# Third mixer: attention units from the ninth tile's slot, the last value tile projected in halves, sinks and first turned copies by ScalarE

## The chip, the core and the metric

The kernel runs on one core of a Trainium2 chip. The metric is the device time of one execution in microseconds (us), median of several; the profile is of one execution.

## What is computed

Four decoder layers over 512 tokens of width 1024 in float32. Each adds a token mixer and then a gated FFN to the residual stream. The change touches only layer 3's mixer, sliding-window attention with sinks (16 query heads, 4 key and value heads of 64, window 128):

```python
q = _partial_rope(_rmsnorm(q, q_norm), cos, sin)
k = _partial_rope(_rmsnorm(k, k_norm), cos, sin)
scores = jnp.einsum('bnqhgd,bnkhd->bnhgqk', qb, kw) * (hd ** -0.5)
scores = jnp.where(mask[None, :, None, None], scores, -jnp.inf)
m = jnp.maximum(jnp.max(scores, axis=-1, keepdims=True), sink)
p = jnp.exp(scores - m)
denom = jnp.sum(p, axis=-1, keepdims=True) + jnp.exp(sink - m)
o = jnp.einsum('bnhgqk,bnkhd->bnqhgd', p / denom, vw).reshape(bsz, s, nq)
return o.astype(h.dtype) @ w_out
```

## The kernel before

Every float32 product with weights is made of two matmuls: a high part in fp32r (`w1`, `x1` or `y1`) and a low part in bf16 (`w2`, `x2` or `y2`). Weights come in panels of 128 x 1024 by DMA from SyncE into a ring of four; ScalarE makes a panel's high part (line 251), GpSimd its low part in four pieces (line 281), and TensorE uses both. A panel slot's high part is made again when TensorE has used the panel four before it.

The mixer's input projection has 12 tiles of 128 features by 512 tokens, one panel each: two of keys (0, 1), eight of queries (2 to 9), two of values (10, 11). A tile is 8 high matmuls (line 310) and 8 low ones (line 320). VectorE scales it out of PSUM (line 2482, an "eviction"), ScalarE squares it, TensorE makes the sums for the head norm ("stat", line 2329), and VectorE applies the rotary embedding ("rope", lines 2498 to 2504: a shuffle into PSUM bank 4, two products, a sum).

Attention runs in 16 units: unit `un` is query tile `un // 2` and a half `un % 2` of the token blocks. An even unit has one short key range (128 keys), so its scores and turns are smaller. The steps of one unit are
- score: TensorE multiplies queries and keys (line 2345); VectorE masks, scales and takes the maximum in four reductions (line 2531); ScalarE makes four exponentials with their sums (line 2441). VectorE first writes the sinks beside the scores (line 2523).
- weights: VectorE takes the reciprocal of the unit before (line 2509), in the midst of the reductions; GpSimd multiplies by it (line 2564).
- turn: TensorE transposes the rows into banks 7 and 4 (line 2362); ScalarE copies bank 7 (line 2455), VectorE bank 4 (`second`, line 2541).
- pv: TensorE multiplies with the values (line 2381); every second unit ScalarE makes `y1` (`high`, line 2461) and VectorE `y2` (`low`, line 2547).
- early: one matmul pair of the output projection (lines 351 and 359), 14 in all.

Values are first turned by TensorE (`turn_v`, line 2318) and copied by ScalarE (line 2423), which counts `swa_v`. The product of an even unit waits for `swa_v`: unit 0 for one, later even ones for both.

The order is written out by hand in `swa_events`: a list of slots, which each engine walks and from which it takes its own steps. Engines take their steps strictly in that order and wait on semaphores. In slot n stands tile n; the statistics and the rope of a tile stand one slot later. Unit v stands in slot `SWA_FIRST + v`; there its score, the turn of unit v - 2 and the product of unit v - 3. The turn of unit 0 waits for all ropes (`swa_rotated` at 30), as bank 4 holds the ropes' partner rows. Buffers for scores rotate over three; the third shares its space with the rope's scratch `xc`.

## Time and profile before

| | us |
|---|---|
| median of 3 runs | 1725.84 (1725.24 to 1725.88) |
| the profiled execution | 1724.62 |
| its span | 1722.8 |
| TensorE busy | 1685.2 (98%) |
| VectorE, ScalarE, GpSimd busy | 1142.7, 1098.6, 1233.2 |

The third mixer stands from 901 to 1013 us. A timeline lists an engine's instructions in order of time: start and duration in us, engine, line and operation, output and inputs, how many were merged, and in brackets the idle time before and who ended it. Ends of matmuls are modelled and groups overlap by their tails, so prices of TensorE's parts are read from start to start; some matmul records are missing.

### The profile page before, as it was taken

The numbers are of one execution on the slowest core, as the hardware profiler recorded it, in microseconds if no ns is written. First come the engines' busy times: TensorE is split into PE (matmuls) and PEld (weight loads), VectorE is DVE, ScalarE is ACT, GpSimd is POOL, SyncE is SP. The second block draws the span as 40 slices with busy tenths as digits, with TensorE's granted clock in tenths as the row PEclk, the third lists the DMA queues.
The fourth block names the chain that finished last, engine by engine and source line by source line (L and its number), as shares of the span: only waits on it lengthen the run. The fifth ranks groups of instructions, "written<-read, shape, count | busy, mean of one in ns | idle before, by whom it ended". The sixth has DMA issues, their size and how long they took to land.

```text
span 1722.8 us, 26957 instructions
## 1 busy us (share of the span) xinstructions
PE 1685.2 (98%) x9549; PEld 1054.9 (61%) x9708; DVE 1142.7 (66%) x1965; ACT 1098.6 (64%) x1566; POOL 1233.2 (72%) x1776
## 2 busy tenths in 40 slices
PE   7999999999999999999999999999999999999999
PEld 4556666666566556666665666666666665566665
DVE  6986777228888865777328857775248886677720
ACT  7887666456877756666545776665455665866632
POOL 7867777877556648777887657778766554777786
PEclk9999999999999999999999999999999999999999
DMA  7334444546233225444544124444443332444443
GB/s 275 113 99 129 150 149 143 157 149 182 74 98 99 97 86 169 149 147 146 156 144 142 38 69 141 150 149 150 146 133 99 99 99 75 134 147 146 147 155 127
DMA packets 65614, 226.53 MB, mean 131 GB/s; under 512 B 8149, under 2 KB 9045, under 8 KB 65109
## 3 DMA queue, kind: packets, MB, share of 16 engines
q1 hardware_dynamic: 64236, 221.89, 40.9%
q10 hardware_dynamic: 1245, 2.92, 0.6%
q8 instruction: 78, 1.28, 0.3%
q14 instruction: 55, 0.45, 0.1%
HBM read 222.48 MB, written 2.10 MB: 130 GB/s over the span
## 4 chain that ended last, share of the span: by engine, by line
PE 78%; ACT 7%; DVE 7%; issue 3%; POOL 3%; DMA 1%; SPq 0%; DVEq 0%; ACTq 0%; POOLq 0%
PE psum L310 24%; PE psum L320 23%; PE psum L351 13%; PE psum L359 12%; POOL w_rest L281 2%; ACT w_big L251 1%; DVE psum L1670 1%; PE psum L2345 1%; PE psum L2381 1%; ACT psum L1514 1%; ACT L1549 1%; DMA w_panel<-in_ssd_in 1%; ACT L1530 1%; PE psum L2362 1%; DVE arena L1715 1%
## 5 line engine op out<-in xcount | busy, mean ns | idle before, releaser
L281 POOL TENSOR_TENSOR w_rest<-w_panel,w_big 128x256 bf16<-128x256 f32 x1660 | 1170.5, 745 | 415.6 <-ACT w_big L251 415.2
L310 PE MATMUL psum<-x_big,w_big 128*128 128x512 f32 x2248 | 590.8, 409 | 7.6 <-ACT x_big L410 6.2
L251 ACT ACTIVATE w_big<-w_panel 128x1024 fp32r<-128x1024 f32 (+1 forms) x414 | 417.0, 1032 | 181.5 <-PE psum L359 124.0
L320 PE MATMUL psum<-x_rest,w_rest 128*128 128x512 bf16 x2141 | 501.2, 380 | 9.2 <-DVE x_rest L513 1.9
L310 PEld LDWEIGHTS psum<-x_big,w_big 128*128 128x128 f32 x2248 | 418.4, 189 | 117.0 <-issue 14.0
L320 PEld LDWEIGHTS psum<-x_rest,w_rest 128*128 128x128 bf16 x2248 | 205.6, 98 | 267.4 <-issue 41.0
L750 DVE SCALAR_TENSOR_TENSOR psum<-ffn_raw,params,psum 128x512 f32<-128x512 f32 x352 | 264.5, 751 | 7.2 <-ACT psum L704 1.0
L742 DVE TENSOR_TENSOR ffn_raw<-psum,rstd 128x512 f32<-128x512 f32 x176 | 120.4, 686 | 140.8 <-PE psum L320 131.8
L704 ACT ACTIVATE psum<-ffn_raw,params 128x512 f32<-128x512 f32 x176 | 137.3, 782 | 99.9 <-DVE ffn_raw L742 95.6
L580 DVE SCALAR_TENSOR_TENSOR x_resid<-psum,x_resid 128x512 f32<-128x512 f32 x64 | 43.8, 688 | 219.7 <-PE psum L359 211.7
L351 PE MATMUL psum<-g_big,w_big 128*128 128x512 f32 x704 | 183.2, 411 | 0.0
L359 PE MATMUL psum<-g_rest,w_rest 128*128 128x512 bf16 x678 | 158.2, 380 | 1.5
L351 PEld LDWEIGHTS psum<-g_big,w_big 128*128 128x128 f32 x704 | 132.7, 189 | 34.2
L711 ACT ACTIVATE g_big<-psum 128x512 fp32r<-128x512 f32 x88 | 52.8, 600 | 112.2 <-DVE psum L759 112.1
L359 PEld LDWEIGHTS psum<-g_rest,w_rest 128*128 128x128 bf16 x704 | 65.0, 98 | 86.1 <-issue 14.3
L351 PE MATMUL psum<-y_big,w_big 128*128 128x512 f32 x320 | 106.6, 457 | 0.5 <-ACT w_big L251 0.5
L513 DVE SCALAR_TENSOR_TENSOR x_rest<-x_big,psum 128x512 bf16<-128x512 f32 x64 | 44.0, 687 | 90.8 <-ACT psum L414 90.8
L359 PE MATMUL psum<-y_rest,w_rest 128*128 128x512 bf16 x298 | 83.0, 382 | 1.4 <-POOL w_rest L281 0.8
L351 PEld LDWEIGHTS psum<-y_big,w_big 128*128 128x128 f32 x320 | 60.2, 191 | 16.3 <-issue 4.1
L759 DVE TENSOR_TENSOR psum<-psum,ffn_silu_out 128x512 f32<-128x512 f32 x88 | 61.5, 699 | 3.2
L763 DVE SCALAR_TENSOR_TENSOR g_rest<-g_big,psum 128x512 bf16<-128x512 f32 x88 | 59.9, 680 | 2.7 <-ACT g_big L711 2.7
L1670 DVE SCALAR_TENSOR_TENSOR psum<-arena,params,psum 128x512 f32<-128x512 f32 x72 | 54.3, 754 | 10.8 <-ACT psum L1514 9.1
(281 smaller groups left out, 1646.5 us busy)
## 6 DMA issues: line engine op xcount, KB each, us to landing
w_panel<-in_up SPq DMA_DIRECT2D x176, 512.0 KB, 3.5
w_panel<-in_dn SPq DMA_DIRECT2D x64, 448.0 KB, 3.2
w_panel<-in_ssd_in SPq DMA_DIRECT2D x41, 512.0 KB, 3.5
w_panel<-in_dn SPq DMA_DIRECT2D x32, 512.0 KB, 3.5
w_panel<-in_hgrn_in SPq DMA_DIRECT2D x32, 512.0 KB, 3.5
w_panel<-in_lru_in SPq DMA_DIRECT2D x18, 512.0 KB, 3.5
w_panel<-in_ssd_out SPq DMA_DIRECT2D x16, 512.0 KB, 3.4
w_panel<-in_swa_in SPq DMA_DIRECT2D x12, 512.0 KB, 3.4
```

Source lines behind the costliest of these rows:

```text
L251: act.activation(k.w1[:, slot, 0:words], k.w[:, slot, 0:words], ACT.Copy, scale=(SHIFT - 1) / SHIFT).then_inc(k.s("panel_big"), 1)
L281: rest = pool.tensor_tensor(k.w2[:, slot, a], k.w[:, slot, a], k.w1[:, slot, a].bitcast(F32), ALU.subtract)
L310: pe.matmul(out, k.w1[:, slot, q * m:(q + 1) * m], k.x1[:, q, :], start=q == 0, stop=False)
L320: mm = pe.matmul(out, k.w2[:, slot, q * m:(q + 1) * m], k.x2[:, q, :], start=False, stop=q == DT - 1)
L351: pe.matmul(out, k.w1[:, slot, (q - p0) * P:(q - p0 + 1) * P], y1[:, q, :], start=q == 0, stop=False)
L359: mm = pe.matmul(out, k.w2[:, slot, (q - p0) * P:(q - p0 + 1) * P], y2[:, q, :], start=False, stop=q == kt - 1)
L704: act.activation(out, k.ffn_raw[:, j % 2, half, 2:], ACT.Identity, bias=k.p("ffn_conv_b", j + (l * 2 * FF_T + half * FF_T)), scale=k.p("ff ...
L742: dve.tensor_tensor(k.ffn_raw[:, j % 2, half, 2:], k.ps[:, k.bank(job, i), :], k.rstd[:, :], ALU.mult).then_inc(k.s("banks_free"), 1)
L750: dve.scalar_tensor_tensor(out, k.ffn_raw[:, j % 2, half, tap:tap + S], k.p("ffn_conv_w", j + ((l * 3 + tap) * 2 * FF_T + half * FF_T)), o ...
L759: dve.tensor_tensor(out, out, k.ffn_silu[:, j % 2, :], ALU.mult).then_inc(k.s("ffn_gated"), 1)
L763: dve.scalar_tensor_tensor(k.g2[:, j, :], k.g1[:, j, :].bitcast(F32), 1 - SHIFT, k.ps[:, lin_bank(j), :], ALU.mult, ALU.add).then_inc(k.s( ...
L1670: dve.scalar_tensor_tensor(conv, b.raw[:, i % 2, tap:tap + S], k.p("ssd_conv_w", tap * 24 + ch), conv, ALU.mult, ALU.add).then_inc(k.s("ss ...
```

## The change

- `SWA_FIRST` goes from 9 to 8: unit v stands in slot 8 + v. In the first two of these slots the rope comes behind the unit's score instead of ahead of it.
- Value tile 11 has no slot of its own: its high half stands in slot 11, between the scores and the product of a unit, its low half in slot 12. The two value turns stand behind the turns of unit 0 and of unit 2. ScalarE's rounding of the panel behind it (`last_round`) stands at the end of slot 12, just ahead of the second value copy.
- The sinks are written by ScalarE, a unit ahead, at a slot's end, and no longer by VectorE.
- For units 0 to 2 (`SWA_BOTH`) ScalarE makes both turned copies.
- The rope's scratch `xc` moves to the last plane of `y`, and unit 2's reductions no longer wait for all ropes.
- An early step takes its low matmul first and then the high one.
- GpSimd weights unit 0 behind panel 12, unit 1 behind 13, units 2 to 5 behind 14, unit 6 within 15.

```diff
@@ -2200,10 +2200,8 @@
         self.vt = a.take(NC, 256)
         self.vraw = a.take(2, S)
         self.scores = [a.take(2, 2, 260) for _ in range(2)]
-        at = a.at
         self.scores.append(a.take(2, 2, 260))
-        roped = Arena(k, at)
-        self.xc = roped.take(S)
+        self.xc = k.y[:, SSD_T - 1, :]
         self.pt = a.take(2, 2, 4 * P)
         self.cos_q, self.sin_q = a.take(S), a.take(S)
         self.fq = a.take(64)
@@ -2230,7 +2228,8 @@
     return P if m == 0 and blk == 0 else 0
 
 
-SWA_FIRST = 9
+SWA_FIRST = 8
+SWA_BOTH = 3
 SWA_FILL = [0] * 6 + [1] * 8 + [0, 0, 2, 2, 2]
 
 
@@ -2243,26 +2242,29 @@
 
     ev, fill = [], 0
     for slot in range(SWA_FIRST + 19):
-        if slot < SWA_TILES:
+        if slot < SWA_TILES - 1:
             ev.append(("tile", slot, 0))
-        i = slot - 1
+        i, v = slot - 1, slot - SWA_FIRST
         if i == 1:
             ev += [("mean", 0, 0), ("mean", 1, 0)]
         elif 2 <= i < SWA_V:
             ev.append(("stat", i, 0))
-        if 0 <= i < SWA_V:
+        if 0 <= i < SWA_V and v not in (0, 1):
             ev.append(("rope", i, 0))
         if i == 3:
             ev += [("normed", 0, 0), ("normed", 1, 0)]
-        elif i in (SWA_V, SWA_V + 1):
-            ev.append(("turn_v", i, 0))
+        elif i in (SWA_V, SWA_V + 2):
+            ev.append(("turn_v", i - (i > SWA_V), 0))
         if i in (5, 9):
             ev.append(("factor", i // 8, 0))
-        v = slot - SWA_FIRST
         if v == 16:
             ev.append(("scale", 15, 0))
         if 0 <= v < 16:
             ev.append(("score", v, 0))
+        if v in (0, 1):
+            ev.append(("rope", i, 0))
+        if slot in (SWA_TILES - 1, SWA_TILES):
+            ev.append(("last_tile", SWA_TILES - 1, slot - SWA_TILES + 1))
         products = [("pv", v - 3, 0)] if 3 <= v else []
         steps = [("early", (fill + i) // 2, (fill + i) % 2) for i in range(SWA_FILL[v])] if v >= 0 else []
         fill += len(steps)
@@ -2273,6 +2275,10 @@
             ev += [("turn", v - 2, 0), ("copied", v - 2, 0)]
         if 0 <= v < 16:
             ev.append(("others", v, 0))
+        if v < 15:
+            ev += [("sink", v + 1, 0)] if v >= 0 else [("sink", 0, 0)] if slot == SWA_FIRST - 1 else []
+        if slot == SWA_TILES:
+            ev.append(("last_round", SWA_TILES - 1, 0))
         if 3 <= v:
             ev.append(("low", v - 3, 0))
         if 2 <= v < 18:
@@ -2304,6 +2310,14 @@
             in_rest(pe, k, job, i)
         else:
             in_tile(pe, k, job, i, fresh=None if i else 4)
+
+    def last_tile(i, part):
+        if part == 0:
+            in_begin(pe, k, job, i)
+            in_big(pe, k, job, i)
+        else:
+            pe.wait_ge(k.s("panel_split"), k.split(job, i))
+            in_rest(pe, k, job, i)
 
     def mean(i, _):
         pe.wait_ge(k.s("swa_sq"), i + 1)
@@ -2384,11 +2398,17 @@
         mm.then_inc(k.s("swa_pv"), 1)
 
     def early(t, o):
+        panel = out_panel("swa_out", o, 0)
+        out, slot, at = k.ps[:, k.bank("swa_out", o), :], k.slot("swa_out", panel), slice(t * P, (t + 1) * P)
         pe.wait_ge(k.s("swa_y_split"), t + 1)
-        out_steps(pe, k, "swa_out", o, t, t + 1, k.y1, k.y2)
-
-    do = {"tile": tile_, "mean": mean, "turn_v": turn_v, "stat": stat, "score": score, "turn": turn, "pv": pv,
-          "early": early}
+        pe.wait_ge(k.s("panel_split"), k.split("swa_out", panel))
+        pe.wait_ge(k.s("banks_free"), k.free("swa_out", o))
+        pe.matmul(out, k.w2[:, slot, at], k.y2[:, t, :], start=t == 0, stop=False)
+        pe.wait_ge(k.s("panel_big"), k.rounds(k.panel0["swa_out"] + panel))
+        pe.matmul(out, k.w1[:, slot, at], k.y1[:, t, :], start=False, stop=False)
+
+    do = {"tile": tile_, "last_tile": last_tile, "mean": mean, "turn_v": turn_v, "stat": stat, "score": score,
+          "turn": turn, "pv": pv, "early": early}
     for what, i, o in swa_events():
         if what in do:
             do[what](i, o)
@@ -2453,6 +2473,21 @@
         act.wait_ge(k.s("swa_turned0"), un + 1)
         skip = swa_keys(un % 2, 0)
         act.activation(b.pt[:, un % 2, 0, skip:], k.ps[:, 7, skip:], ACT.Copy).then_inc(k.s("swa_pt0"), 1)
+        if un < SWA_BOTH:
+            act.wait_ge(k.s("swa_turned1"), un + 1)
+            act.activation(b.pt[:, un % 2, 1, skip:], k.ps[:, 4, skip:], ACT.Copy).then_inc(k.s("swa_pt1"), 1)
+
+    def sink(un, _):
+        t = un // 2
+        if un >= 3:
+            act.wait_ge(k.s("swa_turned1"), un - 2)
+        act.wait_ge(k.s("swa_setup"), 5)
+        at = 8 * (t // 4) + t % 4
+        sinks = b.sinks[:, at:at + 5:4].unsqueeze(2).unsqueeze(3).to_broadcast([P, 2, 2, 1])
+        act.activation(b.scores[un % 3][:, :, :, 256:257], sinks, ACT.Copy).then_inc(k.s("swa_sunk"), 1)
+
+    def last_round(i, _):
+        round_ahead(act, k, job, i)
 
     def high(un, _):
         if un % 2:
@@ -2460,8 +2495,8 @@
             act.wait_ge(k.s("swa_pv"), un + 1)
             act.activation(k.y1[:, t, :], swa_y_bank(k, t), ACT.Copy, scale=1 / SHIFT).then_inc(k.s("swa_y_hi"), 1)
 
-    do = {"tile": tile_, "mean": mean, "turn_v": turn_v, "factor": factor, "score": score, "copied": copied,
-          "high": high, "others": others}
+    do = {"tile": tile_, "last_round": last_round, "mean": mean, "turn_v": turn_v, "factor": factor,
+          "score": score, "copied": copied, "high": high, "others": others, "sink": sink}
     for what, i, o in swa_events():
         if what in do:
             do[what](i, o)
@@ -2513,14 +2548,10 @@
 
     def score(un, _):
         t, m, s = un // 2, un % 2, b.scores[un % 3]
+        at = 8 * (t // 4) + t % 4
         if un >= 3:
             dve.wait_ge(k.s("swa_turned1"), un - 2)
-        elif un == 2:
-            dve.wait_ge(k.s("swa_rotated"), 3 * SWA_V)
         dve.wait_ge(k.s("swa_setup"), 5)
-        at = 8 * (t // 4) + t % 4
-        sinks = b.sinks[:, at:at + 5:4].unsqueeze(2).unsqueeze(3).to_broadcast([P, 2, 2, 1])
-        dve.tensor_copy(s[:, :, :, 256:257], sinks).then_inc(k.s("swa_sunk"), 1)
         dve.wait_ge(k.s("swa_scored"), un + 1)
         dve.wait_ge(k.s("swa_fq"), t // 4 + 1)
         for blk in range(2):
@@ -2533,7 +2564,13 @@
                                          b.sinks[:, at + 4 * a:at + 4 * a + 1], ALU.add, ALU.min,
                                          b.neg[:, m, n:n + 1]).then_inc(k.s("swa_max"), 1)
 
+    def last_tile(i, part):
+        if part:
+            tile_(i, 0)
+
     def second(un, _):
+        if un < SWA_BOTH:
+            return
         if un >= 2:
             dve.wait_ge(k.s("swa_pv"), un - 1)
         dve.wait_ge(k.s("swa_turned1"), un + 1)
@@ -2547,8 +2584,8 @@
             dve.scalar_tensor_tensor(k.y2[:, t, :], k.y1[:, t, :].bitcast(F32), 1 - SHIFT, swa_y_bank(k, t),
                                      ALU.mult, ALU.add).then_inc(k.s("swa_y_split"), 1)
 
-    do = {"tile": tile_, "normed": normed, "rope": rope, "score": score, "scale": last, "low": low,
-          "second": second}
+    do = {"tile": tile_, "last_tile": last_tile, "normed": normed, "rope": rope, "score": score, "scale": last,
+          "low": low, "second": second}
     for what, i, o in swa_events():
         if what in do:
             do[what](i, o)
@@ -2568,20 +2605,22 @@
 def swa_between(pool, k, panel):
 
     def between():
-        swa_weighted(pool, k, 3)
+        swa_weighted(pool, k, 6)
 
     return between if panel == 15 else None
 
 
 def swa_gpsimd(pool, k, panel):
 
-    if panel == 13:
+    if panel == 12:
         swa_weighted(pool, k, 0)
+    elif panel == 13:
+        swa_weighted(pool, k, 1)
     elif panel == 14:
-        for un in (1, 2):
+        for un in range(2, 6):
             swa_weighted(pool, k, un)
     elif panel == 15:
-        for un in range(4, 16):
+        for un in range(7, 16):
             swa_weighted(pool, k, un)
 
 
```

VectorE around the last ropes. In the kernel before, from the end of unit 0's reductions (L2531): the eviction of tile 10, the rope of tile 9, the sinks.

```order
L2531 ISA arena<-psum,arena 128x256
L2531 ISA arena 128x1
L2531 ISA arena<-psum,arena 128x256
L2531 ISA arena 128x1
L2482 TENSOR_TENSOR arena<-psum,rstd 128x512
L2498 STREAM_SHUFFLE psum<-arena 128x512
L2499 TENSOR_TENSOR arena<-arena 128x512
L2501 TENSOR_TENSOR psum<-psum,arena 128x512
L2504 TENSOR_TENSOR arena<-arena,psum 128x512
L2523 COPY arena<-arena 128x4
L2531 ISA arena<-psum,arena 128x256
```

In the changed kernel, from the end of unit 1's reductions (L2562): the rope of tile 8, the eviction of tile 10 (L2517), the rope of tile 9, unit 2's first reduction.

```order
L2562 ISA arena<-psum,arena 128x256
L2562 ISA arena 128x1
L2533 STREAM_SHUFFLE psum<-arena 128x512
L2534 TENSOR_TENSOR y_plain<-arena 128x512
L2536 TENSOR_TENSOR psum<-psum,arena 128x512
L2539 TENSOR_TENSOR arena<-y_plain,psum 128x512
L2517 TENSOR_TENSOR arena<-psum,rstd 128x512
L2533 STREAM_SHUFFLE psum<-arena 128x512
L2534 TENSOR_TENSOR y_plain<-arena 128x512
L2536 TENSOR_TENSOR psum<-psum,arena 128x512
L2539 TENSOR_TENSOR arena<-y_plain,psum 128x512
L2562 ISA arena<-psum,arena 128x128
```

Unit 1's reductions have moved from behind the last rope to ahead of the last two.

TensorE from tile 9's statistics, in slot 10, to the first steps of units 0 to 3. Before: L2329 the statistics, L2345 scores, L310 and L320 tile 11, L2318 a value turn, L2362 the turn of unit 0.

```order
L2329 MATMUL psum<-arena,x_sq 32x2 x16
L2345 MATMUL psum<-arena 128x256 x4
L310 MATMUL psum<-x_big,w_big 128x512 x8
L320 MATMUL psum<-x_rest,w_rest 128x512 x8
L2318 MATMUL psum<-consts,arena 128x128 x4
L2345 MATMUL psum<-arena 128x128 x2
L2345 MATMUL psum<-arena 128x256 x2
L2362 MATMUL psum<-consts,arena 128x128 x6
L2318 MATMUL psum<-consts,arena 128x128 x4
L2345 MATMUL psum<-arena 128x256 x4
```

In the changed kernel: L2343 the statistics, L2359 scores, L2376 the turn of a unit, L2332 a value turn, L2395 a product.

```order
L2343 MATMUL psum<-arena,x_sq 32x2 x16
L2359 MATMUL psum<-arena 128x128 x2
L2359 MATMUL psum<-arena 128x256 x2
L2376 MATMUL psum<-consts,arena 128x128 x6
L2332 MATMUL psum<-consts,arena 128x128 x4
L2359 MATMUL psum<-arena 128x256 x4
L310 MATMUL psum<-x_big,w_big 128x512 x8
L2395 MATMUL psum<-arena 64x128 x6
L2376 MATMUL psum<-consts,arena 128x128 x8
L2359 MATMUL psum<-arena 128x128 x2
L2359 MATMUL psum<-arena 128x256 x2
L320 MATMUL psum<-x_rest,w_rest 128x512 x8
```

Tile 11 stood between the statistics and the turn of unit 0; its halves now stand behind that turn.

ScalarE around the second value copy. Before: L251 a panel's high part, L2423 a value copy, L2441 exponentials, L2455 the copy of bank 7.

```order
L251 ACTIVATE w_big<-w_panel 128x1024
L2423 ACTIVATE arena<-psum 128x4x128
L2441 ACTIVATE arena<-arena 128x129 x2
L2455 ACTIVATE arena<-psum 128x384
L2441 ACTIVATE arena<-arena 128x257 x2
L2423 ACTIVATE arena<-psum 128x4x128
L2441 ACTIVATE arena<-arena 128x257 x3
L2455 ACTIVATE arena<-psum 128x512
```

In the changed kernel, in slot 12: L2461 exponentials, L2496 the high part of y, L2475 and L2478 the copies of both banks, L2487 the sinks, L2443 the value copy.

```order
L2461 ACTIVATE arena<-arena 128x129 x2
L2496 ACTIVATE y_big<-psum 128x512
L2475 ACTIVATE arena<-psum 128x384
L2478 ACTIVATE arena<-psum 128x384
L2461 ACTIVATE arena<-arena 128x257 x2
L2487 ACTIVATE arena<-arena 128x4
L251 ACTIVATE w_big<-w_panel 128x1024
L2443 ACTIVATE arena<-psum 128x4x128
L2461 ACTIVATE arena<-arena 128x257 x3
```

The second value copy now stands behind the high part of y, two copies, the sinks and a panel's high part.

## Rows read from the trace of the kernel before

**Rows 1.** Busy time of each engine in a stretch, units in step.

```profile
core 0: us, PE busy (x) PEld busy (x) DVE busy (x) ACT busy (x) POOL busy (x), PEclk, DMA share, GB/s
...
968.85:995.85 27.00, 26.38 (x247) 19.16 (x249) 23.22 (x93) 21.77 (x78) 13.92 (x32) 1.00 0.01 3
```

**Rows 2.** Timeline of TensorE, ramp from tile 9 to unit 3's product.

```profile
939.72 2.11 PE L310 MATMUL psum<-x_big,w_big 128*128 128x512 f32 x8
...
943.87 0.93 PE L2345 MATMUL psum<-arena 64*128 64x128 f32 x8
944.73 2.11 PE L310 MATMUL psum<-x_big,w_big 128*128 128x512 f32 x8
...
948.51 0.43 PE L2329 MATMUL psum<-arena,x_sq 128*32 128x2 f32 x32
...
954.45 0.93 PE L2345 MATMUL psum<-arena 64*128 64x128 f32 x8
955.31 0.88 PE L2362 MATMUL psum<-consts,arena 128*128 128x128 f32 x6
956.02 0.60 PE L2318 MATMUL psum<-consts,arena 128*128 128x128 f32 x4
957.32 1.13 PE L2345 MATMUL psum<-arena 64*128 64x256 f32 x8 [0.70 <-DVE arena L2531]
958.38 0.88 PE L2381 MATMUL psum<-arena 128*64 128x128 f32 x12
...
968.00 0.93 PE L2345 MATMUL psum<-arena 64*128 64x128 f32 x8 [1.27 <-DVE arena L2531]
968.85 1.09 PE L2381 MATMUL psum<-arena 128*64 128x128 f32 x16
```

**Rows 3.** Timeline of TensorE, units 4 to 8 in step.

```profile
972.26 0.88 PE L2381 MATMUL psum<-arena 128*64 128x128 f32 x12
973.07 0.49 PE L351 MATMUL psum<-y_big,w_big 128*128 128x512 f32 x1
...
973.63 1.04 PE L2362 MATMUL psum<-consts,arena 128*128 128x128 f32 x8
974.60 0.93 PE L2345 MATMUL psum<-arena 64*128 64x128 f32 x8
975.61 1.10 PE L2381 MATMUL psum<-arena 128*64 128x128 f32 x16
```

**Rows 4.** Timeline of VectorE in the ramp.

```profile
939.46 0.69 DVE L2482 TENSOR_TENSOR arena<-psum,rstd 128x512 f32<-128x512 f32 x1 [0.90 <-PE psum L320]
...
947.36 0.40 DVE L2531 CUSTOM_DVE_ANT_0 arena<-psum,arena 128x128 f32<-128x128 f32 x1
...
948.95 0.68 DVE L2482 TENSOR_TENSOR arena<-psum,rstd 128x512 f32<-128x512 f32 x1
...
949.56 0.68 DVE L2498 STREAM_SHUFFLE psum<-arena 128x512 f32<-128x512 f32 x1
...
952.08 0.16 DVE L2523 COPY arena<-arena 128x4 f32<-128x4 f32 x1
...
954.12 0.69 DVE L2482 TENSOR_TENSOR arena<-psum,rstd 128x512 f32<-128x512 f32 x1
...
955.43 0.41 DVE L2531 CUSTOM_DVE_ANT_0 arena<-psum,arena 128x128 f32<-128x128 f32 x1 [0.41 <-PE psum L2345]
...
964.60 1.34 DVE L2523 COPY arena<-arena 128x4 f32<-128x4 f32 x1
```

**Rows 5.** Timeline of ScalarE in the ramp.

```profile
954.78 1.05 ACT L251 ACTIVATE w_big<-w_panel 128x1024 fp32r<-128x1024 f32 x1
...
962.92 0.57 ACT L2461 ACTIVATE y_big<-psum 128x512 fp32r<-128x512 f32 x1
963.40 0.47 ACT L2455 ACTIVATE arena<-psum 128x384 f32<-128x384 f32 x1
963.77 0.50 ACT L2441 ACTIVATE arena<-arena 128x257 f32<-128x257 f32 x1
```

## What the change was predicted to do

> **What bounds the kernel now.** The first view to read is the table of busy time by stretch: over the 27.0 us in which the eight middle units of the third mixer run, TensorE is busy 26.38, VectorE 23.22 and ScalarE 21.77, at a granted clock of 1.00 [rows 1]. TensorE is the bound there, and only its waits can be shortened. The second view is TensorE's timeline over the ramp, from the first projection tiles to the fourth unit's product [rows 2], read by the starts of its groups, since the ends of matmuls are modelled. It gives the price of every part: tile 3.78 (944.73 to 948.51); statistics of a tile 0.37 (939.72 to 943.87 less a tile); scores of an even unit 0.86 (954.45 to 955.31), of an odd one 1.06 (957.32 to 958.38); the turn of an even unit 0.71 (955.31 to 956.02), of a value tile 0.53 (the 0.60 of row 956.02 less the tail that overlaps). From the units in step [rows 3] come the product of an even unit 0.81 (972.26 to 973.07), the turn of an odd one 0.97 (973.63 to 974.60), the product of an odd one 1.03 (the 1.10 of row 975.61 less its tail) and one early step 0.56 (973.07 to 973.63). The third view is VectorE's timeline [rows 4], the fourth ScalarE's [rows 5]: they say what TensorE waits for.
>
> **What the ramp loses before.** From unit 0's scores at 943.87 to unit 3's product at 968.85 lie 24.98 us. The parts in it are two tiles, one statistics, four even and three odd scores, two even and two odd turns, two value turns, two even products and one odd: 7.56 + 0.37 + 3.44 + 3.18 + 1.42 + 1.94 + 1.06 + 1.62 + 1.03 = 21.62. So TensorE loses 3.4 us there, of which 1.27 in one piece before row 968.00 [rows 2]; it follows the sinks' copy that took VectorE 1.34 instead of 0.16 [rows 4]. This 3.4 us is nearly all that starting earlier can give back. The page of the Trainium skill titled "SBUF — State Buffer", section "Who interferes with whom", says that such a copy on VectorE and a GpSimd instruction lock each other out of a shared port; by it the 1.34 is such a lock and is gone with the copy. The 1.34 against 0.16 would agree, and the piece is inside the 3.4 in any case.
>
> **Units one slot earlier.** Up to the statistics of tile 7 nothing changes, and tile 9's first matmul stood at 939.72 [rows 2]; there unit 0's scores now begin. TensorE needs 0.86 + 3.78 + 0.37 + 1.06 + 3.78 + 0.37 + 0.86 = 11.08 from there to the end of unit 2's scores, 950.80. Next in its queue is the turn of unit 0, which waits for all ropes, since the turned scores and the ropes' partner rows share PSUM bank 4. VectorE's prices [rows 4]: four reductions of an even unit 1.59 (947.36 to 948.95), an eviction 0.61 (948.95 to 949.56), a rope 2.52 (949.56 to 952.08), an odd unit's reductions with the reciprocal 1.97 (952.08 to 954.12 less 0.07 for the sinks); an even unit's reductions start 0.98 after its scores (955.43 against 954.45). Now it has tile 8's eviction from 939.46, then waits for the scores to 940.70; reductions to 942.29; rope 7 to 944.81; eviction 945.42; unit 1's reductions, which wait for scores that start at 944.73 and take 1.06, begin about 945.9 and end 947.9; rope 8 to 950.4, eviction 951.0, rope 9 to 953.55. TensorE can turn unit 0 at about 953.7, having been ready at 950.8: **a new wait of 2.9 us**. Before, rope 9 was done at 952.08 and the turn came at 955.31, behind tile 11, so this wait was covered by 3.8 us of projection that the change moves behind it. Bounds: 2.5 if every start on VectorE comes 0.1 sooner, 3.2 if the reductions see 0.1 more each.
>
> Unit 2's reductions stand behind rope 9: 953.55 + 1.59 + 0.09 = 955.2. TensorE has turned unit 0 and value tile 10 by 953.7 + 0.71 + 0.53 = 954.9, and waits **0.4** for them. From 955.35: scores 956.4, first half of tile 11 958.4, product 959.2, turn 960.2, scores 961.0, second half 962.8, product 963.85. No wait shows in this stretch: VectorE's four reductions of unit 3 (2 us from 956.5) and ScalarE's exponentials fit beside the half tile.
>
> **ScalarE in slot 12.** The eleventh value tile's turned copy is what unit 2's product waits for (swa_v at 2). It stands behind, in ScalarE's order: y high part 0.48 (962.92 to 963.40), two copies of 0.37 (963.40 to 963.77), two exponentials of 0.49 (the 0.50 of row 963.77), the sinks, one rounding of a panel at 0.95 (row 954.78, 1.05 less its overlap), and itself, 0.48 for the same shape as the high part [rows 5]. The first of them waits for unit 1's product, 963.85. The sinks on ScalarE have no row; their bounds are 0 and the 0.48 of a copy of 512 columns, and I take 0.15, near the 0.16 that VectorE needs undisturbed. Sum 0.48 + 0.74 + 0.98 + 0.15 + 0.95 + 0.48 = 3.78, so 967.7. TensorE is ready after 0.71 + 0.53 + 1.06, at 966.15: **a wait of 1.6** (1.4 to 2.0). "ScalarE: Activation LUTs", section "What ACT_TABLE_LOAD costs", in the Trainium skill prices an ACTIVATE with immediate scale at 186 ns and 0.833 ns a column, of which 93 ns overlap; a copy of 4 columns would be about 0.10 by that estimate, and the sum 0.05 less.
>
> Before, this copy was issued behind unit 0's, long ahead of its use. With 0.1 for unit 3's second copy, which VectorE still makes, the ramp now waits 2.9 + 0.4 + 1.6 + 0.1 = 5.0 against 3.4: **+1.6**. Splitting tile 11 puts one more change of operand type into the stream, 0 to 0.2; I take 0.1. So **+1.7**.
>
> **Early steps, low half first.** One costs 0.56, where two matmuls in a tile cost 3.78 / 8 = 0.47; the new order can save 0 to 0.09 each, as the shorter load then stands uncovered. Eight stand alone between units: 0.7. The six at the end stand in pairs where TensorE waits for copies anyway, so they give nothing. Ahead of an odd unit's product TensorE already waits 0.15 for VectorE's copy (974.60 to 975.61 less 0.86) [rows 3], which stays, and where TensorE comes sooner it waits a little longer. I take **-0.5** (0 to -0.8).
>
> **Sinks and copies.** On VectorE the sinks' copy ran while it waited for scores, and removing it gives nothing in step. ScalarE has 27.00 - 21.77 = 5.2 us idle over eight units, 0.65 a unit [rows 1]; 0.15 fits. The three second copies on ScalarE (two of 0.37 and one of 0.48) lie in its waits, but for the one counted in slot 12. GpSimd's order (rests of panels 13 to 15 between weightings) asks for unit 5's and 6's weights about as late as before; no wait, 0 to 0.5.
>
> **Sum.** +1.7 - 0.5 = **+1.2 us**. The profiled execution took 1724.62, so it would be 1725.8; the median of the runs shown stands 1.22 above it, so I put the forecast on the median: 1725.84 + 1.2 = **1727.0**. With the bounds, 1726.0 to 1728.2. A measurement here can tell 0.2%, 3.45 us, from no change.
>
> **Rivals.**
> (a) The ramp does close: VectorE reaches rope 9 in time and ScalarE's copy is early enough. For it: 3.4 us of waits are there and sinks leave a VectorE that is nearly full. Against: 2.9 us of projection is no longer between rope and turn. Price: -3.4 and the steps' -0.5 at most, 1721.9; with half of the new waits left, 5.0 / 2 - 3.4 - 0.5 + 0.1 = -1.3, 1724.5. Chance 0.14, centred on 1723.5.
> (b) No net effect: the waits only change their place, as TensorE is the bound on both sides of the ramp. Ramp 0, steps -0.5: 1725.3. It also covers the early steps saving nothing and the rope wait at 2.0. Chance 0.16.
> (c) Slower: ScalarE becomes the bound in step, because it takes one more instruction a unit. It decides from 0.65 us for the sinks [rows 1]. At 0.9, between the 0.16 and 1.34 that VectorE showed [rows 4], twelve units lose 0.25 each, 3.0, and the time is 1727.0 + 3.0 = 1730.0. Against it: it copies four columns. Chance 0.08.
>
> **How the numbers follow.** Forecast 0.62, (a) 0.14, (b) 0.16, (c) 0.08. The range 1724.2 to 1728.9 holds the forecast, (b) and the near part of (a), and leaves out about 0.1 below and 0.08 above. Faster by over 0.2%, below 1722.4, is only the far end of (a): 0.06. Slower, above 1729.3: (c) and a tail, 0.09. Within: 0.85.
>
> **What would show it.** In the changed kernel's TensorE timeline: the first turn preceded by a wait on VectorE's rope of 2.5 to 3.2 us; unit 2's product preceded by 1.4 to 2.0 us on ScalarE's value copy; a single early step of 0.47 to 0.50; the sinks on ScalarE near 0.15 with idle time left beside them. It is wrong if the turn waits under 1 us, if the value copy ends before unit 5's scores, or if ScalarE has no idle time in step.

## The result, and the profile of the changed kernel

| us | kernel before | changed kernel |
|---|---|---|
| median | 1725.21 (15 runs, 1724.62 to 1726.54) | 1729.72 (15 runs, 1727.76 to 1731.10) |
| ratio of the times | | 1.0023 (95%: 1.0016 to 1.003) |
| the profiled execution, its span | 1724.62, 1722.8 | 1728.26, 1726.4 |
| stretch from unit 0's slot to the output projection (below) | 73.53 | 78.27 |

The change costs 4.5 us where 1.2 were forecast; the time lies 0.8 above the range. The ratio's interval goes from 0.16% to 0.30%, so a slowdown of over 0.2% is likely but not certain. It stands in one stretch, which is used from here on as the measure: from the place where unit 0's scores or, before, tile 9 begin (939.72 in [rows 2]; 938.89 now) to TensorE's first group of eight matmuls of the output projection (1013.25 before, 1017.16 now). It is 4.74 longer. The two profiled executions differ by 3.64 only, as the changed one was 0.8 shorter ahead of the stretch and 0.3 shorter behind it, where TensorE's order of steps is the same in both. Such shifts of up to two microseconds ahead of the stretch are seen in the experiments' kernels too, so its length says more than the instants do. The changed kernel's profiled execution is one of its faster ones (1728.26 against a median of 1729.72), so what it shows may be less than the usual loss.

TensorE's timeline of the changed kernel, the answer to [rows 2, 3] (start, duration, engine, line, operation, tiles, in brackets the idle time ahead):

```profile
938.89 0.93 PE L2359 MATMUL psum<-arena 64*128 64x128 f32 x8
...
949.10 0.93 PE L2359 MATMUL psum<-arena 64*128 64x128 f32 x8
953.19 1.51 PE L2376 MATMUL psum<-consts,arena 128*128 128x128 f32 x6 [3.17 <-issue]
954.49 1.06 PE L2332 MATMUL psum<-consts,arena 128*128 128x128 f32 x4
955.49 2.08 PE L2359 MATMUL psum<-arena 64*128 64x256 f32 x8
957.49 2.83 PE L310 MATMUL psum<-x_big,w_big 128*128 128x512 f32 x8
960.25 0.88 PE L2395 MATMUL psum<-arena 128*64 128x128 f32 x12
...
969.86 0.88 PE L2395 MATMUL psum<-arena 128*64 128x128 f32 x12 [1.69 <-ACT arena L2443]
...
972.70 1.09 PE L2395 MATMUL psum<-arena 128*64 128x128 f32 x16
973.73 0.39 PE L2406 MATMUL psum<-y_rest,w_rest 128*128 128x512 bf16 x1
...
974.19 0.82 PE L2376 MATMUL psum<-consts,arena 128*128 128x128 f32 x6
...
1017.16 2.22 PE L351 MATMUL psum<-y_big,w_big 128*128 128x512 f32 x8
```

Both forecast waits are there: 3.17 ahead of unit 0's turn (L2376 at 953.19; "issue" means that the profile names no releaser, and VectorE's rows below do) and 1.69 ahead of unit 2's product, for ScalarE's value copy (969.86). What was not forecast stands between them. The same parts take longer than at their prices of before: the turn of unit 0 takes 1.30 from start to start (0.71 before), the value turn 1.00 (0.53), unit 3's scores 2.00 (1.06), the half tile 2.76, where the same eight matmuls take 2.05 in an experiment below (958.08 to 960.13). That is 0.59 + 0.47 + 0.94 + 0.71 = **2.7 us** more, without a single wait in it. The table of stretches (busy time and count of each engine, then the granted clock of TensorE, DMA share, GB/s) shows why:

```profile
938.89:949.96 11.07, 11.07 (x129) 6.68 (x120) 10.11 (x30) 8.21 (x24) 7.61 (x13) 1.00 0.31 99
949.96:953.19 3.23, 0.06 (x3) 0.03 (x1) 3.19 (x7) 0.34 (x2) 1.25 (x2) 0.85 0.30 75
953.19:960.25 7.06, 7.06 (x26) 5.12 (x26) 3.56 (x18) 4.87 (x18) 5.82 (x12) 0.58 0.20 60
960.25:972.70 12.45, 10.67 (x99) 7.37 (x99) 5.74 (x21) 9.10 (x29) 3.89 (x9) 1.00 0.08 32
972.70:1017.16 44.46, 43.12 (x388) 30.89 (x389) 31.18 (x111) 29.76 (x108) 22.02 (x48) 1.00 0.04 14
```

In the wait TensorE is busy for 0.06 of 3.23 us, and the granted clock falls; in the 7.06 us behind it the mean is 0.58, so the engine ran mostly at 1.2 GHz instead of 2.4; then it is back at 1.00. Read in finer stretches, the clock is at 0.50 from 952.25, within the wait, to 959.03, in the midst of the half tile: 6.8 us, in 5.8 of which TensorE had work. The second wait, 1.69 us within the fourth row, leaves the clock at 1.00. The page "TensorE: Matmul & The Clock Gate" of the Trainium skill, section "HAM oscillation — how this bites in real kernels", states that a wait in mid-kernel can take the clock down to half and that the matmuls behind it pay; by that page the forecast lacked a term, and this trace agrees, with 2.7 us.

So the ramp (to unit 3's product, 972.70) takes 33.81 against 29.13 (939.72 to 968.85 in [rows 2]): +4.68. The parts in it are the same before and after, 25.8 at the prediction's prices, so the loss was 3.4 and is 8.0: 3.17 and 1.69 of waits, 2.7 of clock, and 0.5 in small pieces. Of these, 0.10 is the split of tile 11 (2.05 + 1.83 instead of 3.78) and 0.15 stands ahead of unit 3's product (971.69 to 972.70 less 0.86); the rest is under 0.1 each. Without the clock the ramp is 2.0 longer, where the forecast had 1.7. From there to the output projection it is 44.46 against 44.40, where the forecast had -0.5.

VectorE around the last rope, the answer to [rows 4], and ScalarE in slot 12, the answer to [rows 5]:

```profile
952.40 0.69 DVE L2539 TENSOR_TENSOR arena<-y_plain,psum 128x512 f32<-128x512 f32 x1
953.00 0.40 DVE L2562 CUSTOM_DVE_ANT_0 arena<-psum,arena 128x128 f32<-128x128 f32 x1
```

```profile
965.91 0.60 ACT L2496 ACTIVATE y_big<-psum 128x512 fp32r<-128x512 f32 x1 [1.25 <-PE psum L2395]
...
968.18 0.20 ACT L2487 ACTIVATE arena<-arena 128x4 f32<-128x4 f32 x1
968.27 1.05 ACT L251 ACTIVATE w_big<-w_panel 128x1024 fp32r<-128x1024 f32 x1
969.22 0.59 ACT L2443 ACTIVATE arena<-psum 128x512 f32<-128x512 f32 x1
```

The rope of tile 9 ends at 953.1 and the turn follows at 953.19. The turn also waits for GpSimd's weights of unit 0, but these were done at 948.0, so the rope is what held it. The sinks on ScalarE last 0.20 and hold the next instruction up by 0.09. In step, the answer to [rows 1] is

```profile
974.66:1001.64 26.98, 26.15 (x252) 19.23 (x249) 22.43 (x85) 22.29 (x86) 16.84 (x38) 1.00 0.07 21
```

ScalarE has 4.7 of 27 us left, VectorE 4.6: neither became the bound. This window lies 2 us behind the one of eight units, 972.70 to 999.52, in which ScalarE has 4.8 of 26.8 us left and VectorE 4.4.

### The profile page after: what moved, and what is told of

The parts are those of the page before. It is cut to its first block, busy times and chain, and to the rows that moved or that the text cites. A ratio compares the mean times of both kernels' runs of the same rounds, so it can differ in the third digit from the quotient of the medians.

```text
span 1726.4 us, 27139 instructions
## 1 busy us (share of the span) xinstructions
PE 1698.4 (98%) x9708; PEld 1056.8 (61%) x9708; DVE 1138.1 (66%) x1946; ACT 1101.4 (64%) x1585; POOL 1234.5 (72%) x1776
## 3 DMA queue, kind: packets, MB, share of 16 engines
q8 instruction: 78, 1.28, 0.3%
## 4 chain that ended last, share of the span: by engine, by line
PE 82%; ACT 7%; DVE 6%; issue 3%; POOL 1%; DMA 0%; SPq 0%; DVEq 0%; ACTq 0%; POOLq 0%
PE psum L310 25%; PE psum L320 25%; PE psum L351 13%; PE psum L359 12%; ACT w_big L251 1%; DVE psum L1670 1%; PE psum L1900 1%; PE psum L2395 1%; PE psum L2359 1%; ACT psum L1514 1%; PE psum L2376 1%; ACT L1549 1%; PE psum L1945 1%; DVE arena L1715 1%; ACT psum L1549 0%
## 5 line engine op out<-in xcount | busy, mean ns | idle before, releaser
L310 PE MATMUL psum<-x_big,w_big 128*128 128x512 f32 x2248 | 591.6, 409 | 7.0 <-ACT x_big L410 6.1
L251 ACT ACTIVATE w_big<-w_panel 128x1024 fp32r<-128x1024 f32 (+1 forms) x414 | 417.0, 1032 | 180.5 <-PE psum L359 124.0
L320 PE MATMUL psum<-x_rest,w_rest 128*128 128x512 bf16 x2248 | 521.6, 381 | 1.9 <-DVE x_rest L513 1.9
L310 PEld LDWEIGHTS psum<-x_big,w_big 128*128 128x128 f32 x2248 | 419.0, 189 | 116.9 <-issue 13.9
L320 PEld LDWEIGHTS psum<-x_rest,w_rest 128*128 128x128 bf16 x2248 | 205.7, 98 | 267.4 <-issue 41.3
L359 PE MATMUL psum<-g_rest,w_rest 128*128 128x512 bf16 x704 | 161.7, 380 | 0.0
L351 PE MATMUL psum<-y_big,w_big 128*128 128x512 f32 x306 | 99.9, 455 | 0.5 <-ACT w_big L251 0.5
```

The source lines that it names most:

```text
L251: act.activation(k.w1[:, slot, 0:words], k.w[:, slot, 0:words], ACT.Copy, scale=(SHIFT - 1) / SHIFT).then_inc(k.s("panel_big"), 1)
L310: pe.matmul(out, k.w1[:, slot, q * m:(q + 1) * m], k.x1[:, q, :], start=q == 0, stop=False)
L320: mm = pe.matmul(out, k.w2[:, slot, q * m:(q + 1) * m], k.x2[:, q, :], start=False, stop=q == DT - 1)
L351: pe.matmul(out, k.w1[:, slot, (q - p0) * P:(q - p0 + 1) * P], y1[:, q, :], start=q == 0, stop=False)
L359: mm = pe.matmul(out, k.w2[:, slot, (q - p0) * P:(q - p0 + 1) * P], y2[:, q, :], start=False, stop=q == kt - 1)
```

## Experiments

Each was timed beside the kernel before on the same chip. "Stretch" is the 73.53 of above, from the one profiled execution of each kernel. The ratios' 95% intervals reach about 0.0009 to either side, which is 1.5 us; the differences of 1 us and less rest on the traces. Chips differ a little (see the column "before"), and the expectations are written in times of earlier runs, so with the last kernels the distance to the kernel before is compared.

| kernel | median | before | ratio (95%) | stretch |
|---|---|---|---|---|
| k1_fill | 1727.78 | 1725.15 | 1.0013 (1.0004 to 1.0022) | 76.05 |
| k5_fill4 | 1728.89 | 1725.35 | 1.0019 (1.001 to 1.0028) | 77.61 |
| k4_copy | 1728.58 | 1725.15 | 1.0017 (1.0008 to 1.0026) | 76.23 |
| k2_half | 1726.12 | 1725.15 | 1.0004 (0.9995 to 1.0013) | 74.78 |
| k3_whole | 1723.94 | 1725.15 | 0.9991 (0.9983 to 1.0) | 72.30 |
| k6_early | 1724.68 | 1725.35 | 0.9995 (0.9987 to 1.0004) | 72.78 |
| k7_sinks | 1725.07 | 1725.35 | 0.9999 (0.999 to 1.0008) | 73.66 |
| k8_best | 1724.01 | 1725.35 | 0.9991 (0.9982 to 0.9999) | 72.35 |
| k9_waits | 1723.04 | 1724.69 | 0.9992 (0.9983 to 1.0001) | 72.65 |
| k10_mix | 1722.54 | 1724.69 | 0.9988 (0.9979 to 0.9997) | 71.68 |
| k11_dve | 1722.13 | 1724.69 | 0.9986 (0.9977 to 0.9995) | 71.33 |
| k12_dummy | 1724.80 | 1725.14 | 0.9998 (0.9989 to 1.0007) | 73.56 |

### Is it the clock? The wait filled with matmuls that nobody reads

The high half of tile 11 is computed once more, ahead of unit 0's turn, into its own bank, which the true one then overwrites. The second kernel has `DT // 2` in both places, four matmuls instead of eight.

```
@@ turn(un), TensorE
+            in_begin(pe, k, job, SWA_TILES - 1)
+            for q in range(DT):
+                pe.matmul(k.ps[:, k.bank(job, SWA_TILES - 1), :], k.w1[:, k.slot(job, SWA_TILES - 1), q * P:(q + 1) * P],
+                          k.x1[:, q, :], start=q == 0, stop=q == DT - 1)
```

> The changed kernel with eight matmuls that compute nothing used (tile 11's high half into its own bank, which the real half then overwrites), put ahead of the turn of unit 0, where TensorE has nothing to do for 3.2 us. They add 2.0 us of work and move no other instruction. Theory A (the long wait lowers TensorE's clock, and the parts behind it run at half rate for 2.7 us): the wait ends at the same time, since VectorE's rope releases it, the granted clock stays at 1.00 and the time falls by about 2.7, to 1727.0. Rival B (the parts behind the wait are slow for another reason, such as their operands or GpSimd beside them): unchanged, 1729.7.

TensorE in this kernel:

```profile
952.06 2.11 PE L2370 MATMUL psum<-x_big,w_big 128*128 128x512 f32 x8
955.32 0.84 PE L2380 MATMUL psum<-consts,arena 128*128 128x128 f32 x6 [1.15 <-issue]
956.00 0.60 PE L2332 MATMUL psum<-consts,arena 128*128 128x128 f32 x4
957.02 1.14 PE L2359 MATMUL psum<-arena 64*128 64x256 f32 x8 [0.42 <-DVE arena L2566]
958.08 2.12 PE L310 MATMUL psum<-x_big,w_big 128*128 128x512 f32 x8
960.13 0.88 PE L2399 MATMUL psum<-arena 128*64 128x128 f32 x12
```

The wait is 1.15, every part has its full-rate price again, and the stretch is 2.2 shorter than in the changed kernel although eight matmuls of 2.1 us were added. The wait of 0.42 for unit 2's reductions, which the forecast had and the half rate had covered, is visible. That makes the account: -2.7 for the clock, +0.4 for that wait, +0.1 for the matmuls that don't quite hide. The time fell by 1.9 where 2.7 was expected; the wait of 0.42 was left out of the expectation. The granted clock over the span is 1.000 in all eleven runs, and 0.998 or 0.999 in all fifteen of the changed kernel.

> As the run with eight unused matmuls ahead of unit 0's turn, with four of them: the work between the same end of unit 2's scores and the same release is halved, so TensorE waits some 2.1 us instead of 3.2 (none added) or 1.15 (eight). What stands open is how the half rate sets in. If it follows any wait of 2 us: parts behind it at half rate, 1729.7. If a wait of 2.1 is still taken at full rate, as the one of 1.7 behind the value copy was: as with eight, 1727.8.

```profile
954.55 0.84 PE L2380 MATMUL psum<-consts,arena 128*128 128x128 f32 x6 [2.07 <-issue]
955.24 0.60 PE L2332 MATMUL psum<-consts,arena 128*128 128x128 f32 x4
956.26 1.91 PE L2359 MATMUL psum<-arena 64*128 64x256 f32 x8 [0.42 <-DVE arena L2566]
958.10 2.92 PE L310 MATMUL psum<-x_big,w_big 128*128 128x512 f32 x8
960.95 0.88 PE L2399 MATMUL psum<-arena 128*64 128x128 f32 x12
```

```profile
953.00:956.00 3.00, 1.28 (x10) 1.07 (x10) 2.96 (x11) 1.12 (x5) 0.69 (x2) 1.00 0.56 175
956.00:958.00 2.00, 1.74 (x8) 1.18 (x8) 0.11 (x2) 2.00 (x8) 2.00 (x5) 0.62 0.00 0
958.00:960.00 2.00, 2.00 (x7) 1.54 (x6) 1.58 (x8) 1.01 (x5) 2.00 (x4) 0.53 0.00 0
```

With a wait of 2.07 the first two parts run at full rate, and the clock falls at 956.5, 1.9 us after the wait has ended, and is at 0.50 to 959.9: scores 1.84 instead of 1.06, half tile 2.85 instead of 2.05, together 1.6 us. The eleven runs here show clocks from 0.998 to 1.000 and times from 1727.54 to 1730.33, so from run to run the loss is larger or smaller, and in some too small for the third decimal. The median lies between the two expectations. A wait shorter by a third is no safe cure.

### The other forecast wait: the second value copy ahead of the panel's rounding

```
@@ swa_events
-        elif i in (SWA_V, SWA_V + 2):
-            ev.append(("turn_v", i - (i > SWA_V), 0))
+        elif i == SWA_V:
+            ev.append(("turn_v", i, 0))
...
         if slot == SWA_TILES:
+            ev.append(("turn_v", SWA_TILES - 1, 0))
             ev.append(("last_round", SWA_TILES - 1, 0))
```

> The changed kernel with ScalarE's second value copy ahead of the rounding of a panel (0.95 us). Theory: unit 2's product waits for that copy, so its wait falls from 1.7 to 0.75 us: 1729.7 - 0.95 = 1728.8. Rival (this wait is given back at the next score or copy): 1729.7.

```profile
953.96 1.22 PE L2377 MATMUL psum<-consts,arena 128*128 128x128 f32 x6 [3.15 <-issue]
954.97 1.06 PE L2333 MATMUL psum<-consts,arena 128*128 128x128 f32 x4
955.96 1.98 PE L2360 MATMUL psum<-arena 64*128 64x256 f32 x8
957.86 2.11 PE L310 MATMUL psum<-x_big,w_big 128*128 128x512 f32 x8
...
968.56 0.88 PE L2396 MATMUL psum<-arena 128*64 128x128 f32 x12 [0.75 <-ACT arena L2444]
```

The wait is 0.75 instead of 1.69: the copy moved past one rounding of 0.95, as priced, and the time fell by 1.1 to 1728.58 where 1728.8 was expected. The rounding was 0.9 us of the 4.5, and no more. Up to 960 this kernel is the changed one, yet the clock was at 0.50 for 3.4 us only (954.3 to 957.7, so it fell just behind the wait and was back ahead of the half tile, 2.04), and it cost 0.30 + 0.46 + 0.84 = 1.6 rather than 2.7. How long the clock stays down differs between two executions of the same instructions. The spread of the changed kernel's runs, 3.3 us, fits that, but shows it only in part: of the kernels whose clock is 1.000 in every run, k3_whole spreads by 1.1 and k2_half by 2.6.

### The cover given back: tile 11 ahead of unit 0's turn again

In the first kernel only its high half, in the second all of it, with the value turn and the last rounding a slot earlier:

```
@@ swa_events, the first
-        if slot in (SWA_TILES - 1, SWA_TILES):
-            ev.append(("last_tile", SWA_TILES - 1, slot - SWA_TILES + 1))
+        if slot in (SWA_TILES - 2, SWA_TILES):
+            ev.append(("last_tile", SWA_TILES - 1, slot // SWA_TILES))
@@ swa_events, the second
-        elif i in (SWA_V, SWA_V + 2):
-            ev.append(("turn_v", i - (i > SWA_V), 0))
+        elif i in (SWA_V, SWA_V + 1):
+            ev.append(("turn_v", i, 0))
...
+        if slot == SWA_TILES - 2:
+            ev += [("last_tile", SWA_TILES - 1, 0), ("last_tile", SWA_TILES - 1, 1)]
...
-        if slot == SWA_TILES:
+        if slot == SWA_TILES - 1:
             ev.append(("last_round", SWA_TILES - 1, 0))
```

> The changed kernel with tile 11's high half moved from behind unit 3's scores to ahead of unit 0's turn; its low half stays. The wait for the last rope falls from 3.2 to 1.2 us. Theory A: 2.0 of the wait is filled by work that was due anyway, and the clock stays up: 1729.7 - 2.0 - 2.7 = 1725.0. Rival B (no clock effect): 1727.7.

> The changed kernel with the whole of tile 11 ahead of unit 0's turn, its turn and the rounding of the panel behind it a slot earlier too. Theory A: the wait for the rope (3.2), the half rate behind it (2.7) and the wait for the second value copy (1.7) all go: 1729.7 - 7.6 = 1722.1, 3 us below the kernel before. Rival C (the time of the ramp is VectorE's, whatever TensorE's order): unit 3's reductions wait for VectorE again, and no more than the half rate is won, 1727.

The half leaves waits of 1.14, 0.42, 0.73 and 1.69 at a clock of 1.00: 1.2 above the kernel before by the stretch. The whole tile leaves none of over 0.72; the waits of the second kernel's ramp:

```profile
957.92 0.88 PE L2395 MATMUL psum<-arena 128*64 128x128 f32 x12 [0.72 <-ACT arena L2443]
...
963.26 1.13 PE L2359 MATMUL psum<-arena 64*128 64x256 f32 x8 [0.32 <-DVE arena L2562]
964.80 0.88 PE L2395 MATMUL psum<-arena 128*64 128x128 f32 x12 [0.40 <-ACT arena L2478]
...
966.89 0.93 PE L2359 MATMUL psum<-arena 64*128 64x128 f32 x8 [0.19 <-DVE arena L2562]
```

Its stretch is 6.0 shorter than the changed kernel's and 1.2 shorter than before. So the change does pay, as long as tile 11 stays between the last rope and the turn; moving it behind turned this gain into the loss. Which part of the change pays is told by two kernels below that both have the early steps' new order and VectorE's sinks: with the units a slot earlier, and the value turns, copies and GpSimd's order that go with it (k11_dve), the stretch is 71.33, without (k6_early) 72.78. Both kernels of this section came out slower than expected (by 1.1 and 1.8 us). By the stretch it is 1.2 and 1.6, and new waits in the ramp account for it: 0.42 and 0.73 in the first kernel, the four above, 1.6 in all, in the second.

### The rest of the change, one part at a time

The kernel before with the early steps' order alone changed, and with the sinks alone moved to ScalarE (with `xc` moved, since it shared its place):

```
@@ early(t, o), TensorE
-        out_steps(pe, k, "swa_out", o, t, t + 1, k.y1, k.y2)
...
+        pe.matmul(out, k.w2[:, slot, at], k.y2[:, t, :], start=t == 0, stop=False)
+        pe.wait_ge(k.s("panel_big"), k.rounds(k.panel0["swa_out"] + panel))
+        pe.matmul(out, k.w1[:, slot, at], k.y1[:, t, :], start=False, stop=False)
```

> The kernel before with nothing changed but the early steps, low matmul first. Theory: a step alone between units falls from 0.56 to 0.46 us, eight times 0.10, but TensorE then waits the longer for maxima and copies, so nothing is left: no change, 1725.2. Rival (the term of the forecast, -0.5): 1724.6.

```
@@ score(un, _), VectorE
-        elif un == 2:
-            dve.wait_ge(k.s("swa_rotated"), 3 * SWA_V)
...
-        dve.tensor_copy(s[:, :, :, 256:257], sinks).then_inc(k.s("swa_sunk"), 1)
@@ sink(un, _), ScalarE, a unit ahead
+        act.activation(b.scores[un % 3][:, :, :, 256:257], sinks, ACT.Copy).then_inc(k.s("swa_sunk"), 1)
```

> The kernel before with the sinks written by ScalarE a unit ahead, and the rope's scratch moved, and nothing else. Theory: in step ScalarE has room for the 0.09 us; in the ramp the wait of 1.27 us that followed VectorE's copy of 1.34 goes, and those on VectorE's reductions shrink by some 0.3 each: 1725.2 - 1.5 = 1723.7. Rival (VectorE's order is full in the ramp, so the time comes back at the next reduction): 1725.2.

The early steps' order makes two units take 6.55 instead of 6.75 and the part of the stretch behind unit 3's product 43.63 instead of 44.40: -0.8, although by the times alone the interval holds no change. So the theory of no gain was wrong, and its rival, the forecast's term, came out. The sinks' move takes 0.7 out of the ramp, where the 1.27 wait behind the stretched copy is gone, and puts 0.8 into the steps: 45.23 instead of 44.40. Together +0.1, where 1723.7, a gain, was expected. Of the 0.8, a part comes from a single place: one pair of units takes 7.10, as VectorE's first reduction stands 1.74 behind its scores there and TensorE waits 0.31 for it. Added, the two make -0.77 + 0.83 = +0.06 behind the ramp, and the changed kernel has just that, 44.46 against 44.40.

The stretched copy of the kernel before (964.60, 1.34 in [rows 4]) lies beside this work of GpSimd:

```profile
964.50 1.41 POOL L281 TENSOR_TENSOR w_rest<-w_panel,w_big 128x256 bf16<-128x256 f32 x2
```

It ended at 965.94, as GpSimd's two pieces did (965.91). The other sinks' copies of that kernel agree: the ten of 0.16 ran while GpSimd was idle, and the six of 0.22 to 1.34, this one among them, all overlapped its work.

Where do 0.8 us come from, if an instruction is taken away from VectorE? The distance from an odd unit's scores on TensorE to VectorE's first reduction shows it. In the kernel before (TensorE, then VectorE):

```profile
977.94 1.13 PE L2345 MATMUL psum<-arena 64*128 64x256 f32 x8
```

```profile
978.59 0.16 DVE L2523 COPY arena<-arena 128x4 f32<-128x4 f32 x1
979.13 0.54 DVE L2531 CUSTOM_DVE_ANT_0 arena<-psum,arena 128x256 f32<-128x256 f32 x1 [0.37 <-PE psum L2345]
```

With the sinks on ScalarE:

```profile
977.07 1.13 PE L2345 MATMUL psum<-arena 64*128 64x256 f32 x8
```

```profile
978.46 0.54 DVE L2536 CUSTOM_DVE_ANT_0 arena<-psum,arena 128x256 f32<-128x256 f32 x1 [0.49 <-PE psum L2345]
```

1.19 became 1.39, and for even units 0.97 became 1.17. VectorE's queue has four semaphore waits ahead of a unit's first reduction: `swa_turned1`, `swa_setup`, `swa_scored`, `swa_fq`. The copy stood behind the first two. Taken away, all four stand in a row in front of the reduction. This was the theory for the next runs ("theory D" in their expectations). The page "Perfetto Trace Analysis" of the Trainium skill, section "Identifying Dependency Chains", notes that an instruction that waits on several engines may have semaphore instructions with the further conditions placed ahead of it. It gives no price; here the waits are written out one by one, and the distance grew by 0.2 us.

### Fewer waits, and a copy that nobody reads

```
@@ score(un, _), VectorE, the sinks on ScalarE as above
-        dve.wait_ge(k.s("swa_setup"), 5)
+        if un == 0:
+            dve.wait_ge(k.s("swa_setup"), 5)
...
+        if un % 8 == 0:
+            dve.wait_ge(k.s("swa_fq"), t // 4 + 1)
         dve.wait_ge(k.s("swa_scored"), un + 1)
-        dve.wait_ge(k.s("swa_fq"), t // 4 + 1)
```

> The kernel before with the sinks on ScalarE, and besides VectorE's reductions wait for fewer semaphores: the one for the scale and sink set-up only at unit 0, the one for the query factors only at units 0 and 8 and ahead of the one for the scores. In the run with the sinks alone moved, the first reduction of a unit started 0.20 us later after its scores (1.17 and 1.39 against 0.97 and 1.18), and two units in step took 6.74 to 7.10 against 6.75. Theory D (the copy used to take the waits ahead of the reduction; without it they queue in front of it, some 0.1 each, behind the last one to come): the distance returns to 0.97 and 1.18 or less, two units in step take 6.75 and the time is 1724.3. Rival (VectorE starts late because the copy kept it awake, or because ScalarE writes the same rows): the distance stays 1.17 and 1.39.

```
@@ score(un, _), VectorE, the sinks on ScalarE as above, all four waits
         dve.wait_ge(k.s("swa_setup"), 5)
...
+        dve.tensor_copy(s[:, :, :, 258:259], sinks)
         dve.wait_ge(k.s("swa_scored"), un + 1)
```

> The kernel before with the sinks by ScalarE and the scratch moved, as in the run with these two alone (1725.07), and with a copy on VectorE that nobody reads: the same 4 columns to unused columns beside the scores, in the place where VectorE's sinks' copy stood, between the two first waits and the two last ones of a unit. Theory D (an instruction between the waits takes the first ones, so that the first reduction starts as soon as the scores are there): the first reduction stands 0.97 behind an even unit's scores and 1.18 behind an odd one's, as in the kernel before, and not 1.17 and 1.38; two units take 6.75 everywhere; from unit 3's product to the output projection's first group 44.4 and not 45.2. Such a copy may be stretched by GpSimd, as the 1.34 was, and bring back a part of the 1.27 in the ramp, so 1724.3 (1723.8 to 1725.2). Rival (it is not the copy's presence, but that ScalarE now writes the sinks): the distances stay at 1.17 and 1.38, and the time at 1725.1 or above.

With two waits fewer (a unit's scores, then its first reduction, from two views):

```profile
976.66 1.14 PE L2345 MATMUL psum<-arena 64*128 64x256 f32 x8
```

```profile
977.96 0.54 DVE L2538 CUSTOM_DVE_ANT_0 arena<-psum,arena 128x256 f32<-128x256 f32 x1 [0.45 <-PE psum L2345]
```

With the unread copy:

```profile
977.72 1.14 PE L2345 MATMUL psum<-arena 64*128 64x256 f32 x8
```

```profile
978.37 0.16 DVE L2530 COPY arena<-arena 128x4 f32<-128x4 f32 x1
978.90 0.54 DVE L2538 CUSTOM_DVE_ANT_0 arena<-psum,arena 128x256 f32<-128x256 f32 x1 [0.37 <-PE psum L2345]
```

Two waits fewer bring 1.30, half of the way back. They also bring more time than expected: 1.65 below the kernel before, where theory D had 1.05 (1724.3 against 1725.35), with a stretch 0.9 shorter: 1.1 won in the ramp, where the copy of 1.34 and the wait of 1.27 are gone, and 0.2 lost behind it. The unread copy brings 1.18, all of it: its part behind the ramp is 44.40 again, two units take 6.75, and the stretched copy of 1.34 and the wait of 1.28 are back in the ramp as well, so that the stretch is 73.56, the kernel before to 0.03. ScalarE writes the sinks in this kernel too; so it is not who writes them that matters, but that a copy stands there. That it helps by standing among the waits is shown for half of the 0.2 only. With two waits fewer, two stand in a row ahead of the reduction (`swa_turned1` and `swa_scored`), and in the kernel before, behind the copy, also two (`swa_scored` and `swa_fq`), yet the distances are 1.30 and 1.19: the number of waits in a row does not tell the two apart. The other half stays open, and with it the rival that a copy just ahead keeps VectorE ready; a run without `swa_turned1`, or with the copy ahead of all four waits, was not made.

### Towards a version that beats both

```
@@ k8_best, against k3_whole (and SWA_BOTH = 0)
-        elif i in (SWA_V, SWA_V + 1):
+        elif i == SWA_V + 1:
...
+        if i == SWA_V - 1:
+            ev.append(("turn_v", i + 1, 0))
```

> The kernel with the whole of tile 11 ahead of unit 0's turn, and besides the first value copy on ScalarE ahead of unit 2's last exponentials and all copies of bank 4 by VectorE again. There TensorE waited 0.72 for that value copy and 0.40 for ScalarE's copy of bank 4. Theory: both waits go, 1723.9 - 1.1 = 1722.8. Rival (the exponentials behind the value copy come later and unit 3's maxima hold TensorE instead): 1723.9.

The value copy's wait of 0.72 went, and one of 0.95 on VectorE's second copy came ahead of unit 2's product: nothing gained (a stretch of 72.35 against 72.30; 1724.01 where 1722.8 was expected). With `SWA_BOTH` at 3 again and the waits cut as in k9_waits:

> The run with the first value copy early, but with ScalarE's second copies for units 0 to 2 as in the change and VectorE's waits cut as in the run above. VectorE's copy had kept unit 2's product 0.95 us, ScalarE's kept it 0.40. Theory D: the wait falls to 0.4 and two units in step to 6.55, 1724.0 - 0.55 - 0.6 = 1722.9. Rival: 1723.5, the copy alone.

It came out 2.15 below the kernel before, where 2.45 was expected, and not by the way that was expected: unit 2's product waited 1.06 for ScalarE's second copy and not 0.4. The gain of 0.7 in the stretch over k8_best comes from behind the ramp (44.00 against 44.80), and the ramp is no shorter (27.68 against 27.55).

And k3_whole with the sinks' copy given back to VectorE, in its old place:

> The kernel with the whole of tile 11 ahead of unit 0's turn, with the sinks written by VectorE as before. Theory D: the first reduction comes 0.97 and 1.18 us after the scores again, two units in step take 6.55 instead of 6.64 and 6.77, and the ramp keeps what it had unless a sinks' copy meets GpSimd: 1723.9 - 0.7 = 1723.2. Rival E (where the sinks are written matters in the ramp, where one of VectorE's copies took 1.34 us): slower than 1723.9, by up to 1.2.

Both beat the kernel before with an interval that leaves out no change (so does k8_best, barely), and the second is the best of all: 1722.13 against 1724.69, 2.6 below, where 1.95 was expected. The intervals of the last two overlap, so which of them is the faster rests on the stretches. Against k3_whole its ramp is 0.5 shorter (27.38 against 27.84) and the part behind it 0.5 (43.95 against 44.46); most reductions are back at 0.97 and 1.18. The price of the copy is seen too. Once in the steps it is stretched to 0.72, the reduction behind it begins 1.30 behind its scores (972.67), and these two units take 6.73 from scores to scores where the others take 6.52 to 6.59:

```profile
973.34 0.72 DVE L2556 COPY arena<-arena 128x4 f32<-128x4 f32 x1
973.97 0.40 DVE L2564 CUSTOM_DVE_ANT_0 arena<-psum,arena 128x128 f32<-128x128 f32 x1
```

## Why the prediction was right or wrong

- **The rope wait** (2.9, 2.5 to 3.2): right, 3.17, at the end of its bounds. The ropes took 2.59 to 2.69 instead of 2.52, and unit 0's reductions began 1.08 behind its scores instead of 0.98.
- **The wait for unit 2's reductions** (0.4): right in its mechanism; 0.42 in k1_fill, and hidden behind the half rate in the changed kernel. That all forecast waits together came to 5.0, as forecast (3.17 + 1.69 + 0.15), is partly luck: this one was missing and the first was longer.
- **The second value copy** (1.6, 1.4 to 2.0): right, 1.69; k4_copy takes 0.94 of it away with the rounding.
- **The step that failed** is the way the parts behind the rope wait were priced. "TensorE has turned unit 0 and value tile 10 by 953.7 + 0.71 + 0.53 = 954.9", and the scores and the half tile after it, used durations from rows at a granted clock of 1.00 behind a wait of 3 us, for which the kernel before had no counterpart: once it has begun, its longest wait of TensorE is 1.27. The term is missing from the sum: 2.7 in the profiled execution, 1.6 in k4_copy's, 0 where the wait is filled. It belonged into the bounds at least, since the trace of before did not exclude it. None of the three signs of being wrong that the prediction names came up: they look at the waits, and the waits were right.
- **Early steps** (-0.5, 0 to -0.8): -0.8 where they stand alone, at the end of the range. A single one takes 0.46 (973.73 to 974.19), as "0.47 to 0.50" had it.
- **Sinks**: the price on ScalarE was near (0.15 against 0.20, of which 0.09 hold the engine), but "removing it gives nothing in step" was wrong. It moves VectorE's first reduction of a unit in step back by 0.2 us and costs 0.8 over the steps, and that took the early steps' gain away: this part of the forecast was 0.6 too low. In the ramp its removal is worth 0.7 (k7_sinks), within the forecast's 3.4.
- **Rivals.** (c) gave the slower side, with ScalarE as the bound; that did not come about ([rows 1] and its answer). (a) did not either, since the cover of 3.8 us was moved away; k3_whole, where it stays, shows that the gain behind (a) was there, about 1.2. The side itself, slower by over 0.2%, had a chance of 0.09, and too little, because no case held a cost that a wait leaves behind it. (b) did not come about: the ramp grew by 4.7 and the part behind it stayed.
- **The base.** The forecast stood on a median of three runs, 1725.84; of fifteen it is 1725.21. On that base the forecast would be 1726.4, and the miss is 3.3 and not 2.7.

By its parts, then: +2.0 for waits, the split and small pieces (forecast +1.7), +2.7 for the clock (not forecast), -0.8 and +0.8 for early steps and the sinks' place (forecast -0.5 and 0; their sizes are those of the kernels that have them alone): 4.7 in the stretch, 4.5 in the medians.

## What to carry to other kernels

Price a new wait of TensorE with what follows it: here 3.2 us of idling were followed by 7 us at a mean clock of 0.58, and filling the wait with matmuls that nobody reads made the kernel 1.9 us faster. Before a block of work is moved out of a slot, ask which wait it covers there; tile 11 covered the last rope, and back in its place the same change is a gain. Before a tiny instruction is taken off an engine that is idle anyway, measure the distance to the instruction behind it: here taking it away moved that one by 0.2 us in every unit and cost 0.8 in all, and of two ways to win that back, giving the copy its place again won all of it and dropping waits half.

## What the runs showed of the hardware that was not expected

- The clock's fall depends on more than the length of the last wait: with 3.17 us it came within the wait, 2.2 us from its start, with 3.15 us 0.3 us behind its end, with 2.07 us (and 0.42 behind it) 1.9 us behind its end, and with 1.15 and 1.69 us not at all.
- In the same instructions the clock was at 0.50 for 6.8 us in one profiled execution and for 3.4 in another (k4_copy). The times of these two kernels spread by 3.2 and 3.3 us, those of the kernels at a clock of 1.000 by 1.0 to 2.6.
- With four semaphore waits in a row in VectorE's queue and no copy among them, the reduction behind them began 0.2 us later (0.56 in one unit of k7_sinks). An unrelated copy of 4 columns among them took the 0.2 away, two waits fewer took away 0.1; the cause of the other 0.1 is not shown.
- A copy of 4 columns on VectorE took 0.16 us while GpSimd was idle and 0.22 to 1.34 beside its work in the kernel before, 0.72 in one place of k11_dve; it made TensorE wait 1.27 in one place and delayed a reduction by 0.3 in another. The rule of the Trainium skill's page "SBUF — State Buffer" that the prediction named, a port that VectorE and GpSimd lock against each other, agrees with the copy of 1.34 that ended with GpSimd's work. The 1.34 vanished with the copy and came back with an unread one in its place; the port itself no trace shows.
